# One more unit between logits and transposes in the attention pipeline of a two-block kernel

## What is computed

```python
# forgetting attention, per head, per block of 128 queries
logits = q @ k.T * scale + (cum_q - cum_k); mask causal
out = softmax(logits) @ v
# sparse attention, per head: three branches, gated and summed
out = g0 * cmp(q, kc, vc) + g1 * causal(q, ks, vs) + g2 * causal(q, kw, vw)
```

## Time and profile before

| | |
|---|---|
| median of 3 runs | 1720.78 us (1719.75 to 1722.82) |
| profiled execution | 1723.53 us, span 1721.8 us, mean granted clock 0.98 |
| PE busy | 1632.2 us, 95% |
| DVE busy | 1073.1 us, 62% |
| ACT busy | 828.2 us, 48% |
| POOL busy | 170.4 us, 10% |

### The profile page before, as it was taken

One profiled execution on the slowest core, in us unless ns is written; L12 is line 12 of the kernel. 1 busy time (PEld: TensorE's weight loads), 2 busy tenths in 40 slices (PEclk: granted clock), 3 DMA queues, 4 the chain that ended last, 5 costly groups with the idle time before them and its releaser, 6 DMA issues.

```text
span 1721.8 us, 31639 instructions
## 1 busy us (share of the span) xinstructions
PE 1632.2 (95%) x12986; PEld 1591.5 (92%) x12986; DVE 1073.1 (62%) x1557; ACT 828.2 (48%) x1180; POOL 170.4 (10%) x233
## 2 busy tenths in 40 slices
PE   5898999899999899999999999999998989999998
PEld 5898998899999899998999999999997879899998
DVE  7676776687645665566666556665545666666653
ACT  4344545665634544463544444444465445354442
POOL 2002120400201600020100010000100012010000
PEclk9999999999999999999999999999998989999999
DMA  9553591455454454562455464545643004255543
GB/s 369 193 175 120 221 365 52 155 195 197 170 179 165 152 190 160 176 231 98 172 175 191 152 215 173 191 154 179 219 157 142 31 20 152 98 185 177 186 156 123
DMA packets 44837, 293.14 MB, mean 170 GB/s; under 512 B 5168, under 2 KB 6464, under 8 KB 15168
## 3 DMA queue, kind: packets, MB, share of 16 engines
q1 hardware_dynamic: 40896, 265.49, 43.5%
q0 software_dynamic: 3840, 26.23, 3.9%
HBM read 288.02 MB, written 3.67 MB: 169 GB/s over the span
## 4 chain that ended last, share of the span: by engine, by line
PE 74%; DVE 12%; ACT 9%; DMA 2%; issue 2%; POOL 0%; DVEq 0%; ACTq 0%; POOLq 0%
PE G L434 22%; PE G L436 22%; PE G L435 22%; DVE w_lo L1454 4%; ACT w_hi L957 3%; PE O L622 2%; PE T L608 2%; DVE XB L1707 1%; PE L L917 1%; DMA mod_w<-w_ada 1%; DVE X L1574 1%; PE L L810 1%; DVE mod_w L1421 1%; DMA raw<-w_wouta 1%; ACT x_hi L1034 1%
## 5 line engine op out<-in xcount | busy, mean ns | idle before, releaser
L1454 DVE TENSOR_TENSOR w_lo<-raw,w_hi 128x2048 fp32r<-128x2048 f32 (+2 forms) x259 | 546.2, 2113 | 221.1 <-ACT w_hi L957 220.9
L434 PE MATMUL G<-x_hi,w_hi 128*128 128x256 f32 x2176 | 624.9, 287 | 15.1 <-DVE w_lo L1454 10.0
L435 PE MATMUL G<-x_lo,w_hi 128*128 128x256 f32 x2176 | 620.3, 285 | 0.0
L436 PE MATMUL G<-x_hi,w_lo 128*128 128x256 f32 x2176 | 620.0, 285 | 0.0
L957 ACT ACTIVATE w_hi<-raw 128x2048 fp32r<-128x2048 f32 (+1 forms) x261 | 459.3, 1763 | 138.1 <-DMA raw<-w_ffout 43.4
L434 PEld LDWEIGHTS G<-x_hi,w_hi 128*128 128x128 f32 x2176 | 422.3, 194 | 20.2 <-DVE w_lo L1454 11.9
L435 PEld LDWEIGHTS G<-x_lo,w_hi 128*128 128x128 f32 x2176 | 422.2, 194 | 0.1
L436 PEld LDWEIGHTS G<-x_hi,w_lo 128*128 128x128 f32 x2176 | 422.1, 194 | 0.0
L434 PE MATMUL G<-hid_hi,w_hi 128*128 128x256 f32 x1280 | 366.3, 286 | 5.1 <-DVE w_lo L1454 3.1
L436 PE MATMUL G<-hid_hi,w_lo 128*128 128x256 f32 x1280 | 362.7, 283 | 0.0
L435 PE MATMUL G<-hid_lo,w_hi 128*128 128x256 f32 x1280 | 362.6, 283 | 0.0
(11 more groups left out here) (387 smaller groups left out, 1833.1 us busy)
## 6 DMA issues: line engine op xcount, KB each, us to landing
raw<-w_f1in SPq DMA_DIRECT2D x44, 1024.0 KB, 4.8
raw<-w_f2in SPq DMA_DIRECT2D x44, 1024.0 KB, 4.8
raw<-w_f1out SPq DMA_DIRECT2D x32, 704.0 KB, 4.0
raw<-w_f2out SPq DMA_DIRECT2D x32, 704.0 KB, 4.0
raw<-w_ffin SPq DMA_DIRECT2D x16, 1024.0 KB, 4.8
raw<-w_ffout SPq DMA_DIRECT2D x16, 1024.0 KB, 4.8
mod_x<-w_ada POOLq DMA_DIRECT2D x12, 1024.0 KB, 9.0
raw<-w_xk SPq DMA_DIRECT2D x8, 1024.0 KB, 6.1
```

The lines of the kernel that those rows point to most:

```text
L434: mm(out, l_hi, r_hi, start=start, stop=False)
L435: mm(out, l_hi, r_lo, start=False, stop=False)
L436: return mm(out, l_lo, r_hi, start=False, stop=stop)
L1454: v.tensor_tensor(w_lo[b][:, 0:s.size], raw[b][:, 0:s.size], w_hi[b][:, 0:s.size].bitcast(F32), ALU.subtract).then_inc(s_lo, 1)
```

## The change

Transposes move from one step behind QK to two, PV from two to three; the program of each attention has one step more. `ns` and `nw` become one attention `nsw` of 32 heads (64 units), the branch found from the head number; the wait of PE between them goes, and the three weight slots beside them are spread over 64 steps (21, 21 and 22) in place of 16, 16 and 32. DVE takes bank `t` = 0 in step 16k+1 and bank `t` = 1 in step 16k+2, ahead of `beside_`; `rs` has a row for each bank, and the wait for DVE's own product moves from behind the take to ahead of the next one of the same bank. POOL's wait for its own addition comes only when the same part of `AO` is met again. Buffers stay two of each.

```diff
-    "att": ([("fox", 32), ("xa0", 8), ("ns", 32), ("nw", 32), ("xa1", 8)],
+    "att": ([("fox", 32), ("xa0", 8), ("nsw", 64), ("xa1", 8)],
...
-        rs = sb("rs", [P, 8])
+        rs = sb("rs", [P, 2, 8])
...
-                        "ns": [("xv1", 0), ("xv1", 1)], "nw": [("xv1", 2)]}
+                        "nsw": [("xv1", 0), ("xv1", 1), ("xv1", 2)]}
+        beside_steps = {"fox": 2 * H, "nsw": 4 * H}
...
# PE, attention
-                for step in range(len(units) + 2):
+                for step in range(len(units) + 3):
...
-                    if 1 <= step <= len(units):
-                        u = step - 1
+                    if 2 <= step <= len(units) + 1:
+                        u = step - 2
...
-                    if step >= 2:
-                        u = step - 2
+                    if step >= 3:
+                        u = step - 3
...
# PE, call
-            attention("ns", H, HD, lambda t: P * (t + 1), qk_nsa(ks),
...
-            pe.wait_ge(q("ns.o"), nth("ns.o", 4))
-            attention("nw", H, HD, lambda t: P * (t + 1), qk_nsa(kw),
...
+            attention("nsw", 2 * H, HD, lambda t: P * (t + 1), qk_nsa, pv_nsa,
+                      lambda step: share("nsw", step, x_hi, x_lo))
...
# DVE, attention
-                    beside_(step)
-                    if step >= 3 and (step - 1) % (2 * per) == 0:
-                        half = (step - 1) // (2 * per) - 1
-                        for t in range(2):
-
+                    for t in range(2):
+                        if step > 2 and (step - 1 - t) % (2 * per) == 0:
+                            half = (step - 1 - t) // (2 * per) - 1
+                            if half:
+                                dve.wait_ge(q(name + ".o"), nth(name + ".o", 2 * (half - 1) + t + 1))
                             dve.wait_ge(q(name + ".pv"), nth(name + ".pv", 2 * per * (half + 1) - 1 + t))
                             cols = slice(base + t * heads + half * per, base + t * heads + (half + 1) * per)
-                            own(v.reciprocal(rs[:, 0:per], ssum[:, cols]))
+                            own(v.reciprocal(rs[:, t, 0:per], ssum[:, cols]))
                             take(half, t)
-                            dve.wait_ge(q(name + ".o"), nth(name + ".o", 2 * half + t + 1))
+                    beside_(step)
+                dve.wait_ge(q(name + ".o"), nth(name + ".o", 2 * heads // per))
...
# DVE, take of the sparse attention
+            def gated_take(half, t):
+                branch, part = divmod(half, 2)
+                g_ = gates[:, t, 24 * part + branch + 1:24 * part + 24:3]
+                own(v.tensor_tensor(rs[:, t], rs[:, t], g_, ALU.mult))
+                if half:
+                    dve.wait_ge(q("nsa.sum"), 2 * half + t - 1)
+                v.tensor_tensor(h8(Ot[t][:]), h8(O[t][:, :]), heads8(rs[:, t]), ALU.mult).then_inc(q("nsw.o"), 1)
...
# POOL
+            for k in range(8):
+                half, t = divmod(k, 2)
+                half %= 2
+                pool.wait_ge(q("nsw.o"), nth("nsw.o", k + 1))
+                view = AO[:, t, half * 512:(half + 1) * 512]
+                if k >= 4:
+                    pool.wait_ge(q("nsa.sum"), k - 3)
+                g_.tensor_tensor(view, view, Ot[t][:], ALU.add).then_inc(q("nsa.sum"), 1)
```

More of the change, by code:

```diff
@@ L103 @@
         ("f1out1", "mean"): 2, ("f1out1", "root"): 2,
-        ("foxt", "y"): 2, ("xa0t", "y"): 0, ("nsat", "y"): 0, ("xa1t", "y"): 0}
+        ("nsw", "o"): 8, ("foxt", "y"): 2, ("xa0t", "y"): 0, ("nsat", "y"): 0, ("xa1t", "y"): 0}
 SHARED = {}
@@ L323, in build @@
         beside_slots = {"fox": [("wouta", 0), ("wouta", 1), ("wouta", 2)],
-                        "ns": [("xv1", 0), ("xv1", 1)], "nw": [("xv1", 2)]}
+                        "nsw": [("xv1", 0), ("xv1", 1), ("xv1", 2)]}
+        beside_steps = {"fox": 2 * H, "nsw": 4 * H}
         def turn_starts(attention_name):
             count = len(beside_slots[attention_name])
-            return [2 * H * k // count for k in range(count + 1)]
+            return [beside_steps[attention_name] * k // count for k in range(count + 1)]
         def turn_of(attention_name, step):
@@ L912, in _, with qk_nsa, pv_nsa @@
                         .then_inc(q("nc.pv"), 1)
[L914 to L919, removed]
+            def qk_nsa(both, t, bank):
+                branch, h = divmod(both, H)
+                nk = P * (t + 1)
+                return mm(bank[:, 0:nk], qT[:, h // 2, t * P:(t + 1) * P], (ks, kw)[branch][:, h % 2, h // 4, 0:nk],
+                          start=True, stop=True)
+            def pv_nsa(both, c):
+                branch, h = divmod(both, H)
+                return (vs, vw)[branch][:, c, (h // 4) * HD:(h // 4 + 1) * HD]
             pe.wait_ge(q("nc.o"), 4)
@@ L923, in _ @@
             pe.wait_ge(q("nsa.zero"), 2)
-            attention("ns", H, HD, lambda t: P * (t + 1), qk_nsa(ks),
-                      lambda h, c: vs[:, c, (h // 4) * HD:(h // 4 + 1) * HD],
-                      lambda step: share("ns", step, x_hi, x_lo))
-            pe.wait_ge(q("ns.o"), nth("ns.o", 4))
-            attention("nw", H, HD, lambda t: P * (t + 1), qk_nsa(kw),
-                      lambda h, c: vw[:, c, (h // 4) * HD:(h // 4 + 1) * HD],
-                      lambda step: share("nw", step, x_hi, x_lo))
+            attention("nsw", 2 * H, HD, lambda t: P * (t + 1), qk_nsa, pv_nsa,
+                      lambda step: share("nsw", step, x_hi, x_lo))
             gemm_b(st["xv1"], 3, st["xv1"].j0 + 3, x_hi, x_lo)
@@ L1008, in beside @@
                         at[0] += 1
-                ends = [min(start + 1, 2 * H) for start in turn_starts(attention_name)[1:]]
+                ends = [min(start + 1, beside_steps[attention_name]) for start in turn_starts(attention_name)[1:]]
                 if out and u in ends:
@@ L1392, in _ @@
                          ACT.Copy).then_inc(q("nc.o"), 1)
[L1393 to L1396, removed]
+            attention("nsw", 2 * H, lambda t: P * (t + 1), 32,
+                      lambda u: beside("nsw", u, True))
             splits_to(st["xv1"].n0 + 3 + AHEAD)
@@ L1548, in take @@
                                     O[t][:, :].rearrange("p (h d) -> p h d", h=per),
-                                    bc(rs[:, 0:per].unsqueeze(2), [P, per, 512 // per]), ALU.mult)\
+                                    bc(rs[:, t, 0:per].unsqueeze(2), [P, per, 512 // per]), ALU.mult)\
                         .then_inc(q(name + ".o"), 1)
@@ L2002, in _ @@
             dve.wait_ge(q("nc.o"), 4)
[L2003 to L2006, removed]
+            attention("nsw", 2 * H, HD, lambda t: P * (t + 1), causal, 32, gated_take,
+                      lambda step: beside("nsw", step))
             splits_to(st["xv1"].n0 + 3 + AHEAD)
```

## The result

The changed kernel takes 1695.06 us as the median of four runs (1689.22 to 1698.79), the kernel before 1720.26 (1718.57 to 1722.82): a ratio of 0.9849, 95% interval 0.9817 to 0.9881, or 26 us less (20 to 32). I had forecast 1705 with a range of 1699 to 1714. The profiled execution took 1693.66 us.

The account below looks back on a forecast made before the run. PE, busy for 95% of the span, was taken as the bound, so only its waits and slow clock could be won. Sparse attention 9.3 + `fox` 4.7 + cross-attentions 2.0 = 16.0 us off 1720.8, say 1705; range 1699 to 1714.

Parts of the forecast that it names:

- Bound and mechanism: PE bounds; its transposes' waits for ACT's exponential fall from 15.3 us to under 3, waits for `PT` copies come instead.
- Sparse attention: First to last double transposes in `ns` and `nw`: 90.1 us becomes 80.8, 9.3 less.
- Own work with the small `PT` waits: Sparse attention: PE's own work 68.3 us, plus 2.3 us of late `PT` copies in 8 odd steps without a triple.
- The stalls at the takes: Sparse attention: PE waits at three takes, 1.6 + 2.2 + 2.2 = 6.0 us, the longer two with a splitting quarter.
- The clock, 2.5 x 1.7 = 4.2: Sparse attention: slower clock behind both longer take stalls and half of the third, 1.7 us each; bounds 0 to 5.1.
- nearest row: Profile row in the sparse attention before: a 1.70 us PE stall at a take, after which the clock fell.
- The rival that kept the clock: Sparse attention: the level stays at 2.4 GHz through the stalls, 4.2 us more gained, 1701 us; chance 0.13.
- `fox`: Forgetting attention: 2.8 us steady, 1.0 at the start, 0.7 clock, 0.2 at the end; together 4.7 (bounds 2.5 and 6).
- PE's own price: From two equations in `ns` and `nw`: head core 1.61 us, triple 0.40; for `fox` 42.2 us of own work.
- Cross-attentions: Both cross-attentions: 1.0 us less each from filled waits, 2.0 us in all; bounds 0.4 and 1.2 each.
- Takes: DVE's take schedule: second bank's gate product issued at 3.14, held by POOL's addition until 3.88; its reciprocal taken as free.
- Costed at nothing: ACT's splitting quarters, DVE's waits before reusing `rs[t]`, POOL's waits for its sum, transfers and the extra step: no cost.

Follow-up runs that it names:

- again: The changed kernel once more, nothing edited: 1696.28 us, ratio 0.9861 to the kernel before.
- before_rs: The kernel before with only `rs` widened from 8 to 16 columns, moving later SBUF tiles by 32 bytes: 1716.12 us, ratio 0.9989.
- before_rs_two: before_rs a second time (the kernel before, `rs` 16 columns wide): 1714.64 us, ratio 0.998.
- depth_only: The kernel before with only the pipeline deepened, `ns` and `nw` separate, both banks taken in one step: 1700.9 us, ratio 0.9894.
- merge_only: The changed kernel with the old pipeline depth and both banks taken in one step, still 64 units: 1713.1 us, ratio 0.996.
- after_unshifted: The changed kernel with its first `rs` in the old place and the second behind all tiles, so nothing shifts: 1698.13 us, ratio 0.9872.
- after_64: The changed kernel with `rs` 24 columns wide, later tiles 64 bytes further on than in the kernel before: 1688.12 us, ratio 0.9831.
- gates_ahead: The changed kernel with reciprocal and gate product of both banks made ahead of the take of bank 0: 1690.64 us, ratio 0.9843.
- before_again: The kernel before, nothing edited, for a second profile: 1718.45 us, ratio 0.9997.
- before_96: The kernel before with `rs` 32 columns wide, later tiles 96 bytes further on: 1717.44 us, ratio 0.9994.
- before_64: The kernel before with `rs` 24 columns wide, later tiles 64 bytes further on: 1703.92 us, ratio 0.9906.
- before_128: The kernel before with `rs` 40 columns wide, later tiles 128 bytes further on: 1722.42 us, ratio 1.0028.
- gates_quarters_64: gates_ahead with DVE's quarters of weight splitting moved off the takes and `rs` 24 columns wide (64 bytes): 1677.11 us, ratio 0.9764.

## Why the prediction was too small

The 26 us (24 in `again`) come apart as 20.8 in the attentions and about 2.7 from the shifted tiles, the mean of before_rs (1.9 us less, interval 4.6 less to 0.9 more) and before_rs_two (3.4, 0.9 to 6.0). Together 23.5 of 24 to 26. The kernel without the shift confirms the split: 22 us less (19 to 25) with all of the change but that.

**Bound and mechanism: right.** The waits for the exponential went, the new one is PV for `PT`, and depth_only shows that the extra unit does nearly all of it (17.5 of 20.8 us), while merge_only shows that the merge alone does not (1.7).

**Sparse attention: 90.1 to 80.8 forecast, 76.9 measured.** Own work with the small `PT` waits: 68.3 + 2.3 = 70.6 forecast; 76.93 less 4.9 of stalls and 1.7 of clock is 70.3. The stalls at the takes, 1.6 + 2.2 + 2.2 = 6.0 forecast, were 1.88 + 1.79 + 1.20 = 4.9. **The clock, 2.5 x 1.7 = 4.2, is the term that failed**: one fall, 1.7 us. In both executions of the changed kernel one of three stalls had a fall behind it, and not the same one; after_unshifted and after_64, with the same stalls, had one each behind the second. That is 4 falls behind 8 stalls of 1.8 to 1.9 us and none behind 4 of 1.2. With gates_ahead and its stalls of 1.1 us and less there was none. The "nearest row", one fall after 1.70 us, was one draw, and I made it nearly a rule: the same 1.70 us stall stands in seven traces of the kernel before and its shifted copies, with a granted clock of 0.81 over the 8.83 us behind it in four (before, before_again, before_rs_two, before_96) and of 1.00 in three (before_rs, before_64, before_128). Half a fall for each of the two longer stalls would have been 1.7 us. The rival that kept the clock was right for two of the three places. The Trainium skill (TensorE: Matmul & The Clock Gate, Part 1: The HAM clock gate) says that the gate watches activity by a count that runs freely, not tied to the kernel's start; that would let the same stall fare differently from run to run, as it does here, but no run here shows the cause.

**`fox`: 4.7 forecast, 5.9 measured.** The start gave 1.0 (5.59 to 4.63 us from first QK to the first double transposes, the wait down from 2.33 to 0.89), where I had 1.0 + 0.7. The steady part gave 4.9, 45.94 to 41.07, where I had 2.8: 41.07 us is less than the 42.2 that I had called PE's own price, so the price from two equations in `ns` was too high for `fox`, and so was the 0.9 that I left for the take.

**Cross-attentions: 2.0 forecast, 1.6 measured** (16.50 to 15.68, PE busy all of it).

**Takes: right by their steps.** The gate product of bank 1 held for 0.91 us (0.74 by my schedule), one quarter of the splitting behind it, and a free reciprocal. The Trainium skill (SBUF — State Buffer, Who interferes with whom) had no reciprocal among the instructions that contend with GpSimd, and the trace agrees: 0.19 us inside POOL's addition at 1334.80.

**Costed at nothing, wrongly: the wider `rs`.** This is the second step of the forecast that failed. The diff shows it, and I looked at it only for its buffers. It moves the operands of thousands of products. The trace of before couldn't price it, and it should have stood as an unknown in the range; 32 bytes gave some 3 us here, and 64 gave 16 in the kernel before.

**Range.** Its lower end, 1699, took in the clock and `fox` at their best but no scatter of the unchanged stretches. With the terms as measured and no shift, 1720.3 - 20.8 = 1699.5 would have been just inside it.

## What to carry to other kernels

Count the stages from mark to mark by the same instruction in both traces, and set their sum against the difference of the times: what the stages don't hold is in the rest, and there a second look for changed addresses or clock is due. When a diff changes the size of any tile, run the old kernel with that tile size alone, before crediting the schedule; and try a few widths of padding over several executions each, since here 64 bytes were worth 9 to 16 us, and the same kernel drew different paces from one execution to the next. A stall at a take shrinks most by moving short instructions that another engine would hold ahead of what starts that engine.

## What was unexpected of the hardware

- The pace of PE's products depends on where SBUF tiles lie: 286, 285, 282, 286 and 288 ns for `hid_hi` with `w_hi` in the kernel before at 0, 32, 64, 96 and 128 bytes, medians 1718 to 1720, 1715 to 1716, 1704, 1717 and 1722 us. From start to start the `hid` products take 118.8, 117.8, 114.6, 118.3 and 119.9 ns there. It is not all of it: after_64 has 283 and gates_quarters_64 282 ns with the same tiles, since an unbroken run of products takes one of a few fixed lengths, 60.2 or 62.3 us at 64 bytes, in one kernel and even in one execution.
- The same stall may or may not have a lower clock behind it: four of seven times after 1.70 us, four of eight after 1.8 to 1.9 us. Stretches that no edit touched show it too: the compressed branch stood at 0.91 for 18.08 us in one execution and at 0.83 for 19.72 in another.
